# Two-block transformer kernel, one core: where VectorE's steps stand inside the latent and recurrent mixers of the second block

## What is computed

```
z = rmsnorm(h, mix_norm) @ w_in
c_q, c_kv, k_pe, z_u, z_v, hq, hf, hi, hg, rq, rk, rv, rg = split(z)
y_a = mla_mixer(...)               # latent attention
y_b = spatial_gating_mixer(...)
y_c = hgrn2_mixer(hq, hf, hi, hg)  # gated recurrence, 4 heads of key size 128
y_d = retention_mixer(...)
h = h + concat(y_a, y_b, y_c, y_d) @ w_out

mla:   q = rmsnorm(c_q, q_norm) @ w_uq ;  kv = rmsnorm(c_kv, kv_norm) @ w_ukv
       k = [kv's first 64 of each head, rope(k_pe)] ;  v = kv's other 64
       softmax(q k^T, causal) @ v, 4 heads
hgrn2: log_f = log(forget) ;  b = cumsum(log_f) in a chunk
       scores[t,s] = sum_k q[t,k] exp(b[t,k] - b[s,k]) k[s,k]
```

## Time and profile before

| | |
|---|---|
| median of 3 executions | 3040.51 us (3040.47 to 3040.69) |
| the profiled execution's own time | 3041.03 us |
| its span, first to last instruction | 3039.7 us |
| granted TensorE clock, mean | 0.998 |
| PE busy | 3006.6 us (99%) |
| DVE, ACT, POOL busy | 1417.4, 725.0, 2176.7 us |

### The profile page before, as it was taken

The page is one execution under the profiler, slowest core; times in us unless marked ns, Lnnn a source line. Parts: engine busy times, 40 slices in busy tenths (PEclk is TensorE's granted clock), DMA queues, the critical chain, the costliest instruction groups (busy, mean ns, idle before and its releaser), DMA issues.

```text
span 3039.7 us, 39494 instructions
## 1 busy us (share of the span) xinstructions
PE 3006.6 (99%) x14966; PEld 2436.4 (80%) x14966; DVE 1417.4 (47%) x2165; ACT 725.0 (24%) x1438; POOL 2176.7 (72%) x2524
## 2 busy tenths in 40 slices
PE   9999999999999999999999999999999999999998
PEld 7776777888888888887788888888888877888887
DVE  5467556777156421476732212622213767422214
ACT  3433222222021100344411101311002444111003
POOL 6665668988788877754487777877777544877775
PEclk9999999999999999999999999999999999999999
DMA  5322223333333333322133333333333221333332
GB/s 162 79 67 63 77 80 91 97 97 97 99 99 104 97 97 97 92 55 62 56 98 97 97 104 97 91 98 97 98 97 96 64 55 49 104 98 98 104 97 84
DMA packets 469206, 272.92 MB, mean 90 GB/s; under 512 B 20798, under 2 KB 465136, under 8 KB 469016
## 3 DMA queue, kind: packets, MB, share of 16 engines
q1 hardware_dynamic: 466904, 267.22, 29.8%
q10 hardware_dynamic: 2112, 3.17, 0.3%
HBM read 268.21 MB, written 2.12 MB: 89 GB/s over the span
## 4 chain that ended last, share of the span: by engine, by line
PE 87%; DVE 3%; ACT 1%; issue 0%; DVEq 0%; ACTq 0%
PE bank L728 17%; PE bank L729 17%; PE bank L737 17%; PE bank L1270 7%; PE bank L1269 7%; PE bank L1277 7%; PE bank L850 2%; PE bank L858 2%; PE bank L851 1%; PE bank L775 1%; PE bank L776 1%; DVE arena L2421 1%; PE bank L780 1%; PE bank L1122 1%; PE bank L1442 1%; PE bank L885 1%
## 5 line engine op out<-in xcount | busy, mean ns | idle before, releaser
L685 POOL TENSOR_TENSOR wl<-raw,wh 128x256 fp32r<-128x256 f32 x2016 | 1616.4, 832 | 286.4 <-PE bank L737 181.1
L678 POOL TENSOR_SCALAR wh<-raw 128x1024 fp32r<-128x1024 f32 x504 | 563.7, 1118 | 555.9 <-PE bank L729 170.2
L728 PE MATMUL bank<-xh,wh 128*128 128x512 f32 x1552 | 610.7, 393 | 0.0
L729 PE MATMUL bank<-xl,wh 128*128 128x512 f32 x1552 | 604.3, 389 | 0.0
L2421 DVE TENSOR_TENSOR arena<-bank,nrm 128x512 f32<-128x512 f32 (+1 forms) x237 | 152.6, 683 | 542.7 <-PE bank L737 541.1
L737 PE MATMUL bank<-xh,wl 128*128 128x512 f32 x1552 | 390.6, 391 | 0.0
L2421 DVE TENSOR_TENSOR arena<-arena 128x512 f32<-128x512 f32 (+1 forms) x372 | 337.9, 915 | 57.6 <-ACT arena L2105 11.7
L728 PEld LDWEIGHTS bank<-xh,wh 128*128 128x128 f32 x1552 | 291.8, 188 | 62.7 <-issue 2.1
L737 PEld LDWEIGHTS bank<-xh,wl 128*128 128x128 f32 x1552 | 289.9, 188 | 64.5 <-issue 4.6
L729 PEld LDWEIGHTS bank<-xl,wh 128*128 128x128 f32 x1552 | 291.5, 188 | 60.3 <-issue 1.2
L728 PE MATMUL bank<-arena_rounded,wh 128*128 128x512 f32 x816 | 318.6, 390 | 1.0 <-DVE arena L2421 1.0
(11 more groups left out here) (385 smaller groups left out, 4126.1 us busy)
## 6 DMA issues: line engine op xcount, KB each, us to landing
raw<-in_ffn_w_gate SPq DMA_DIRECT2D x176, 256.0 KB, 3.1
raw<-in_ffn_w_up SPq DMA_DIRECT2D x176, 256.0 KB, 3.1
raw<-in_ffn_w_down SPq DMA_DIRECT2D x176, 256.0 KB, 2.9
raw<-in_w_in SPq DMA_DIRECT2D x158, 256.0 KB, 3.1
raw<-in_w_up SPq DMA_DIRECT2D x88, 256.0 KB, 3.1
raw<-in_w_gate SPq DMA_DIRECT2D x64, 256.0 KB, 3.0
raw<-in_w_out SPq DMA_DIRECT2D x48, 256.0 KB, 3.0
raw<-in_w_down SPq DMA_DIRECT2D x44, 256.0 KB, 2.9
```

The lines of the kernel that those rows point to most:

```text
L678: pool.tensor_scalar(wh[:, s, :], raw[:, s, :], 1.0, 0.0, ALU.mult, ALU.add).then_inc(split, 1)
L685: ins = pool.tensor_tensor(wl[:, s, c], raw[:, s, c], wh[:, s, c].bitcast(F32), ALU.subtract)
L728: pe.matmul(psum, cols(wh, i), xhi, start=(i == 0), stop=False)
L729: ins = pe.matmul(psum, cols(wh, i), xlo, start=False, stop=False)
```

## The change

No instruction is added or removed but for four of ACT's copies, which become DVE's (two in each layer). The rest is order:

- `sums(2)` and `sums(3)` move from units 9 and 11 to units 3 and 4.
- The q norm moves from unit 14 to 11 and its remainders from 16 to 13, the kv norm from 15 to 12 and its remainder from 17 to 14; ACT's high parts from 15 and 16 to 12 and 13.
- Of the latent keys ACT copies heads 0 and 1 (from the first bank), DVE heads 2 and 3 (from the second) at the end of its unit 24. PE waits for both parts where it waited for one.
- At the attention's end `lout_rest(7)` stands between the two products on `hgate`.

```diff
@@ -1373,6 +1373,7 @@
 
             def latent_values():
                 s = slab_start(("uv", l))
+                pe.wait_ge(*T.at("evac0", "uk", l))
                 ins = token_major(s, kv_in, piece_cols(256, 512, 256), pieces=1)
                 piece_used(ins, "gemm", "uv", l)
                 done_at["uv", l] = now[0]
@@ -2140,10 +2142,9 @@
                         ins.then_inc(*A.up(*(("evac", "rot", 0, l) if hh == 3 else ())))
                 if done_at["uk", l] == n:
                     s = evac_start(("uk", l))
-                    for hh in range(NH):
-                        ins = act.activation(kh[hh][0:HD, :], bank[2 * s + hh // 2][hh % 2 * HD:hh % 2 * HD + HD, :],
-                                             ACT.Copy)
-                        ins.then_inc(*A.up(*(("evac", "uk", l) if hh == 3 else ())))
+                    for hh in range(2):
+                        ins = act.activation(kh[hh][0:HD, :], bank[2 * s][hh * HD:hh * HD + HD, :], ACT.Copy)
+                        ins.then_inc(*A.up(*(("evac0", "uk", l) if hh else ())))
                 if done_at["uv", l] == n:
                     copy_pair(("uv", l), [a.rearrange("p i d -> p (i d)") for a in mv])
 
@@ -2223,9 +2224,9 @@
                     root(OB[:, :], "ms", f"q{l}")
                 if n == 7:
                     root(OB[:, :], "ms", f"kv{l}", log=hn[:, 0, :], y=hn[:, 1, :])
-                if n == 15:
+                if n == 12:
                     first_parts(f"q{l}", two(cq), op_hi)
-                if n == 16:
+                if n == 13:
                     first_parts(f"kv{l}", [ckv], op_hi[:, 2:, :])
                 if done_at["hi", l] == n - 1:
                     rows_in("hi", hi)
@@ -3076,32 +3077,28 @@
                     s = evac_start(("ckv", l))
                     tt(ckv, bank[2 * s][:, :], hrstd, ALU.mult)
                     tt(kpe, bank[2 * s + 1][64:96, :], hrstd[64:96, :], ALU.mult, "evac", "ckv", l)
-                if n == 2:
-                    sums(1)
-                if n == 9:
-                    sums(2)
-                if n == 11:
-                    sums(3)
+                if n in (2, 3, 4):
+                    sums(n - 1)
                 if lv == 5 and hh < NH - 1:
                     carried(hh + 1)
                 if lv == (4 if hh else 6):
                     states(hh)
                 if n == 5:
                     rstd_first(OB[:, :], (f"q{l}",))
-                if n == 14:
+                if n == 11:
                     rstd_last((f"q{l}",))
                     for i in range(2):
                         stt(cq[:, i, :], cq[:, i, :], g("q")[:, i:i + 1], nrm[:, 1, :], ALU.mult, ALU.mult,
                             "xn", f"q{l}", i)
-                if n == 16:
+                if n == 13:
                     for i in range(2):
                         rest(f"q{l}", i, cq[:, i, :], op_hi[:, i, :], op_lo[:, i, :])
                 if n == 8:
                     rstd_first(OB[:, :], (f"kv{l}",), hn[:, 1, :], gnt[:, 1, :])
-                if n == 15:
+                if n == 12:
                     rstd_last((f"kv{l}",), None, hn[:, 1, :], gnt[:, 1, :])
                     stt(ckv, ckv, g("kv")[:, 0:1], hn[:, 1, :], ALU.mult, ALU.mult, "xn", f"kv{l}", 0)
-                if n == 17:
+                if n == 14:
                     rest(f"kv{l}", 0, ckv, op_hi[:, 2, :], op_lo[:, 2, :])
                 if done_at["hq", 1, l] == n - 1:
                     rows_out(("hq", 1, l), hq[:, 2:4, :])
@@ -3113,6 +3110,11 @@
                     key_rotated()
                 if n - 1 == done_at["uq", 1, l]:
                     query_turns()
+                if n - 1 == done_at["uk", l]:
+                    s = evac_start(("uk", l))
+                    for hh in (2, 3):
+                        v.tensor_copy(kh[hh][0:HD, :], bank[2 * s + 1][hh % 2 * HD:hh % 2 * HD + HD, :])\
+                            .then_inc(*V.up(*(("evac", "uk", l) if hh == 3 else ())))
                 if (hh, lv) == (3, 0):
                     rstd_first(PT[:, :], ("h", 0, l))
                 if n == UNITS - 1:
@@ -3163,10 +3165,10 @@
                     gated_group(1)
                     v.wait_ge(*V.at("hg", l))
                     last()
-                    for c in range(2):
-                        tt(hgate[:, c, :], hgate[:, c, :], hn[:, c, :], ALU.mult, "gout", "h", c, l)
-                if u == 15:
+                    tt(hgate[:, 0, :], hgate[:, 0, :], hn[:, 0, :], ALU.mult, "gout", "h", 0, l)
                     lout_rest(7)
+                    last()
+                    tt(hgate[:, 1, :], hgate[:, 1, :], hn[:, 1, :], ALU.mult, "gout", "h", 1, l)
                 if u == 0:
                     rstd_first(OB[:, :], ("h", 1, l), gnt[:, 1, :], qtmp)
                 if u == 0:
```

## The result

The change made the kernel slower: 3049.18 us against 3040.49 us, medians of eight executions each, a ratio of 1.003 (95% interval 1.0021 to 1.0039), or +8.7 us. The forecast was 3045.5 us, with "within 0.2%" as the likeliest outcome; the time lies inside the range and on the far side of that 0.2%. The profiled execution took 3048.3 us (span 3047.0), 7.3 us more than that of before.

What follows compares the result with a forecast made beforehand. The prediction took PE, busy 99% of the span, as the bound, with VectorE mattering only where PE waits. Its terms 0 + 7.0 - 2.0 + 0 = +5.0 us on the median's 3040.51 made 3045.5 us, range 3038.5 to 3049.5.

Steps and rivals of the forecast that it cites:

- same: Whole kernel: time within 0.2%, 6.1 us, of the kernel before; chance 0.57.
- 6.1 us bound: Whole kernel: the 0.2% that a measurement can tell from no change.
- part 3: Key copies split between ACT and DVE, unit 26: waits shrink, -2.0 us over both layers, bounds -2.8 and +1.0.
- part 2: Latent norms moved earlier: new waits in units 12 and 14, unit 16's gone, +3.5 us per layer, +7.0 in all.
- the forecast's own range: Whole kernel: 3042 to 3048 us, from the bounds of the latent norms' and key copies' terms; forecast's chance 0.53.
- the wider range: Whole kernel: 3038.5 to 3049.5 us, meant to hold 8 in 10.
- Parts 1 and 4: Running sums moved to units 3 and 4, and operand 7's remainder at the attention's end: 0 us each.
- A whole instruction is locked out: Rival, chance 0.07: nine slowed DVE operations each wait for a whole L685, about +2.2 us per layer, 3049.9 us.
- The clock falls for longer: Rival, chance 0.15: the 4.2 us wait leaves TensorE at 1.2 GHz for two stretches, +1.7 us per layer, 3048.9.

Runs made afterwards that it cites:

- keys_dist_first: Kernel before with the key copies split between ACT and DVE, and the distances of unit 26 ahead of DVE's two copies: 3037.56 us, ratio 0.9992.
- after_dist_first: Changed kernel with the distances of unit 26 moved ahead of DVE's two key copies: 3046.55 us, ratio 1.0019 against the kernel before.
- keys_only: Kernel before with only the key copies split between ACT and DVE as in the change: 3040.63 us, ratio 1.0002.
- sums_rest_only: Kernel before with only the running sums in units 3 and 4 and operand 7's remainder moved at the attention's end: 3040.46 us, ratio 1.0000.

## Why the prediction was wrong

**The outcome forecast was "same"; it was slower.** By its own terms: 0 + 7.0 - 2.0 + 0 = +5.0, just under the 6.1 us bound. The trace has 0 + 7.5 + 0.1 + 0 = +7.6 in the mixers, 7.3 in the span, and the medians 8.7. Of the 3.7 us between forecast and medians part 3 makes 2.1 and part 2 0.5; the other 1.1 is not placed. The time lies above the forecast's own range, 3042 to 3048; that the wider range holds it is owed to the room left for two rivals whose sums did not come.

**The step that failed is part 3**, "the pair of unit 26 ready at 1389.4". It failed twice. The pair was laid down with 1.35 us for two operations, though the earlier trace rows showed 2.17 for the same two. POOL was priced for the norms but not here, and POOL's L678, whose start is tied to PE at about 2.3 us behind level 25 (1389.05 - 1386.67 before, 1392.47 - 1390.22 after), lies right across it. And the start at 1388.05 came out 0.3 us late (1391.92, with the whole stretch shifted by 3.55): the copies took 1.41, not 1.30, and the two operations behind them 1.52, not 1.38. VectorE in the changed kernel, then POOL:

```profile
1387.13 1.41 DVE L3116 COPY arena<-bank 64x512 f32<-64x512 f32 x2 [0.51 <-PE bank L737]
1388.58 1.52 DVE L2422 TENSOR_TENSOR arena<-arena 128x512 f32<-128x512 f32 x2
...
1391.92 2.13 DVE L2422 TENSOR_TENSOR arena<-arena 128x512 f32<-128x512 f32 x2
```

```profile
1392.47 1.05 POOL L678 TENSOR_SCALAR wh<-raw 128x1024 fp32r<-128x1024 f32 x1 [4.55 <-PE bank L809]
```

To gain, the pair had to start before L678 by more than one operation; it started 0.55 us before it, and the next one follows 0.6 us behind. From the forecast's own start the lead would have been 1389.05 - 1388.05 = 1.00 us, and 1.35 the right price. The late start took 0.31 of it, and 0.13 went because PE no longer waits for ACT's last two copies behind level 25, so that L678, which waits for PE's L809, came 2.25 us behind that level and not 2.38. Either one alone would have left the lead above 0.6. In keys_dist_first it started 0.72 us before, and the gain came. And after_dist_first, the changed kernel with this one race won, comes to 1.0019, or +5.8 us against the kernel before beside it: inside the 0.2%, though its interval reaches across it.

The prediction had no reason for the difference between the layers before, 1.56 and 0.67. It is the same race, lost in the first and won in the second. Kernel before: POOL in the first layer, then VectorE and POOL in the second:

```profile
1389.05 1.04 POOL L678 TENSOR_SCALAR wh<-raw 128x1024 fp32r<-128x1024 f32 x1 [4.25 <-PE bank L809]
...
2466.28 1.29 DVE L2421 TENSOR_TENSOR arena<-arena 128x512 f32<-128x512 f32 x2 [1.50 <-ACT arena L2172]
...
2466.89 1.59 POOL L678 TENSOR_SCALAR wh<-raw 128x1024 fp32r<-128x1024 f32 x1 [4.28 <-PE bank L809]
```

The pair started 0.58 us before L678 in the first layer (1388.47) and took 2.17; it started 0.61 before in the second and took 1.29. Over both layers of all thirteen kernels of this document, every pair that started up to 0.587 us ahead of L678 had its second operation held (1.53 to 1.56 us), and with every one from 0.594 us on that operation took 0.68 to 0.69. In the changed kernel and in keys_only it started 0.54 to 0.55 us ahead, in both layers.

**Part 2 held.** New waits at 12 and 14, none at 15 and 16: forecast 1.4 and 4.2 us, found 2.05 and 3.92 in the second layer and, with a low clock between, 2.04 and 2.46 in the first; net +3.5 forecast, +3.7 found in each layer. The 0.6 us at level 12 is the pair of unit 12, 2.48 us and not 1.7: POOL's L678 follows its L685 0.16 us behind and meets the pair as well, which I had not laid in.

**Parts 1 and 4 held** at nothing, with the addition that the sums are worth 1 us in each layer when the norms stand behind them; the forecast counted that inside part 2.

**The rivals.** "A whole instruction is locked out" had the right mechanism and too small a chance, 0.07. I had read four L685 in 3.7 us with VectorE's operations between them as evidence of sharing. They are not: two engines that take turns look the same from the sum. Its price, a whole 0.73 on top of 0.69, was wrong: a held operation ended 0.53 us behind the one that held it and not 0.69, so the turns overlap a little, and the 1.1 to 1.2 us that I had taken from the earlier trace rows is already the locked price. What the rival missed is that it bears on part 3. "The clock falls for longer" did not happen: behind level 14 the clock fell once in each layer, as it had behind 16 before, and a second fall behind level 12, in the first layer alone, cost nothing (last section).

**The chances.** The forecast's +5.0 stood 1.1 us from the bound, and of its own terms only the negative one rested on an edge, a start that was 0.25 us from being late. With part 3 at zero, as its own upper bounds allowed, the sum was +7 and the outcome "slower".

## What to carry to other kernels

Where a norm or a copy is moved into another engine's idle time, lay the timeline of the engine that shares its operands' memory over the new place, before the idle time is counted as free. When two operations meet on such a shared path, some hundredths of a microsecond decide which one pays, so a gain that needs one to be first must be reckoned from the start of the other, not from durations. And a unit late on the critical path takes the sum of what stands in its chain: the same 1.35 us of scans was worth 1 us with the norms behind it and nothing without them.

## What the runs showed of the hardware

**VectorE and POOL take turns by whole instructions.** In the changed kernel the pair of unit 26 ends at 1391.92 + 2.13 = 1394.05, and L678 at 1392.47 + 1.05 = 1393.52, 0.53 before. In keys_dist_first L678 started 0.57 us before VectorE's pair ended and took 1.48 us. POOL's L678 reads one operand and holds VectorE as its L685 with two does; VectorE's operations with one operand in a bank are not held: 1.29 us for two from 1337.01, with L685 running from 1337.13. The Trainium skill (SBUF — State Buffer, Who interferes with whom) says that a VectorE instruction with two SBUF inputs contends with a GpSimd one that reads SBUF, and that the order of issue decides who is blocked. The runs agree, with 1.11 us against 256 columns and 1.67 against 512.

**The low clock behind a wait is not given by the wait.** Behind the 2.06 us wait of unit 16 the first layer before was granted 0.50, 1.2 GHz. In keys_only the same wait of 2.06 and 2.07 us stood in both layers, and the clock behind it was this (busy by engine, then granted clock):

```profile
1352.50:1355.90 3.40, 3.40 (x36) 3.23 (x33) 3.20 (x6) 1.75 (x7) 0.00 (x0) 1.00 0.02 5
2428.70:2432.10 3.40, 3.40 (x35) 3.23 (x30) 3.20 (x5) 1.66 (x7) 0.00 (x0) 1.00 0.00 0
```

Levels 10 to 17 then took 29.30 us instead of 30.9. With and without the fall, both unchanged in code: 1.6 us each time. Before, keys_only and sums_rest_only differ in their profiles by how many of these falls they caught, two, none and one. That is one source of the 5 us that executions of one kernel differ by: among the 72 of the kernel before beside the experiments, the six with a mean granted clock of 0.999 took 3036.6 to 3038.7 us and the eleven with 0.997 took 3041.8 to 3042.9. It can be a source of the 1.4 us between the profiled executions and the medians too, but was not separated from others there.

**Behind a wait that is followed by another wait the low clock was free here.** In the changed kernel the wait of level 12 was 2.04 us in the first layer and 2.05 in the second, and this followed, first layer and second:

```profile
1337.45:1340.86 3.41, 3.41 (x23) 2.37 (x21) 3.27 (x6) 0.00 (x0) 0.67 (x1) 0.51 0.01 2
...
2418.00:2421.00 3.00, 3.00 (x39) 2.24 (x34) 2.80 (x5) 0.00 (x0) 0.43 (x1) 1.00 0.27 82
```

Level 14 then waited 2.46 us where PE had been slow and 3.92 where it had not, and levels 10 to 17 took 34.64 and 34.59: VectorE set the time, and PE's clock did not matter. That rests on VectorE's chain being as long in both. With PE slow, POOL's second run of L685 came later and held the q remainders (2.22 us for two) and not the two fused operations of the kv norm (1.42); with PE fast it was the other way round (1.27 and 2.29).
